# The opening of the FFN: where GpSimd forms the third pair's modulation product, and the order of the four gated tiles

## The reference

```
h = rms_norm(x) * (1 + scale) + shift          # scale, shift from ada_w, six vectors a layer
z = h @ w_up                                    # 1024 -> 2 * 3072
u, v = z[..., :3072], z[..., 3072:]
u = depthwise_conv3(u)
f = (gelu(u) * v) @ w_down                      # 3072 -> 1024
x = x + gate * rms_norm(f)
```

## Time and profile before

| | us |
|---|---|
| median of 3 runs | 2104.82 (2103.49 to 2105.01) |
| the profiled execution's own time | 2108.7 |
| its span, first to last instruction | 2106.9 |
| PE busy | 2025.1 (96%) |
| DVE busy | 1517.2 (72%) |
| POOL busy | 1295.8 (62%) |
| ACT busy | 843.0 (40%) |
| mean granted TensorE clock | 0.976 of full speed |

### The profile page before, as it was taken

The page is one execution under the profiler, slowest core; times in us unless marked ns, Lnnn a source line. Parts: engine busy times, 40 slices in busy tenths (PEclk is TensorE's granted clock), DMA queues, the critical chain, the costliest instruction groups (busy, mean ns, idle before and its releaser), DMA issues.

```text
span 2106.9 us, 26627 instructions
## 1 busy us (share of the span) xinstructions
PE 2025.1 (96%) x9048; PEld 1662.4 (79%) x9048; DVE 1517.2 (72%) x1510; ACT 843.0 (40%) x1119; POOL 1295.8 (62%) x836
## 2 busy tenths in 40 slices
PE   6899999999999999999999999799999999999996
PEld 6677776877778888888888768688888888888885
DVE  7588888978677777777777774697656665676557
ACT  4576768446322323232322355473332233222322
POOL 4534244655877877877787462368766676667653
PEclk9999999998999999999999988799999999999998
DMA  7132322531222222222222400211111111111114
GB/s 310 65 115 80 114 80 90 200 141 34 97 90 89 80 90 90 77 88 94 90 70 90 170 31 11 90 51 70 40 50 60 60 43 50 57 60 50 50 40 160
DMA packets 55931, 179.68 MB, mean 85 GB/s; under 512 B 5040, under 2 KB 6352, under 8 KB 55248
## 3 DMA queue, kind: packets, MB, share of 16 engines
q1 hardware_dynamic: 55888, 179.13, 23.8%
HBM read 166.52 MB, written 12.58 MB: 85 GB/s over the span
## 4 chain that ended last, share of the span: by engine, by line
PE 79%; DVE 7%; ACT 7%; issue 3%; POOL 3%; DMA 1%; ACTq 0%; POOLq 0%; SPq 0%; DVEq 0%
PE ps L908 38%; PE ps L587 32%; PE ps L755 3%; PE ps L1023 1%; PE ps L641 1%; PE ps L1060 1%; DVE ps L1979 1%; ACT TH L1237 1%; PE ps L689 1%; DVE sq L1838 1%; DVE Y L1918 1%; DMA ada_first<-ada 1%; ACT RA L1240 1%; ACT TH L1247 1%; ACT L1247 0%
## 5 line engine op out<-in xcount | busy, mean ns | idle before, releaser
L2100 DVE TENSOR_TENSOR Y<-Y,ps 128x1024 f32<-128x1024 f32 x336 | 406.0, 1219 | 35.6 <-PE ps L587 0.2
L1710 POOL TENSOR_TENSOR F_lo<-S,F_hi 128x1024 fp32r<-128x1024 f32 x44 | 107.0, 2431 | 328.4 <-ACT F_hi L1372 328.4
L587 PE MATMUL ps<-F_hi,WC_hi 128*128 128x512 f32 x736 | 231.8, 393 | 4.1 <-DVE Y L2100 1.6
L1124 ACT ACTIVATE So_hi<-So_raw 128x512 fp32r<-128x512 f32 x132 | 82.6, 627 | 374.3 <-POOL So_raw L1585 370.2
L587 PE MATMUL ps<-F_hi,WC_lo 128*128 128x512 f32 x736 | 230.0, 390 | 0.0
L1347 ACT ACTIVATE S<-S 128x1024 f32<-128x1024 f32 x48 | 51.0, 1062 | 442.1 <-DVE S L2204 442.0
L587 PE MATMUL ps<-F_lo,WC_hi 128*128 128x512 f32 x704 | 217.5, 390 | 0.0
L1688 POOL TENSOR_TENSOR So_lo<-So_raw,So_hi 128x512 fp32r<-128x512 f32 x132 | 187.5, 1447 | 6.1 <-ACT So_hi L1124 6.1
L587 PEld LDWEIGHTS ps<-F_hi,WC_hi 128*128 128x128 f32 x736 | 138.4, 189 | 34.8 <-DVE Y L2100 2.4
L587 PEld LDWEIGHTS ps<-F_hi,WC_lo 128*128 128x128 f32 x736 | 138.7, 188 | 29.1
L587 PEld LDWEIGHTS ps<-F_lo,WC_hi 128*128 128x128 f32 x704 | 132.7, 189 | 27.8
(11 more groups left out here) (302 smaller groups left out, 5379.8 us busy)
## 6 DMA issues: line engine op xcount, KB each, us to landing
rawA<-wA SPq DMA_DIRECT2D x62, 512.0 KB, 3.2
rawB<-wB SPq DMA_DIRECT2D x62, 512.0 KB, 3.2
E<-ada SPq DMA_DIRECT2D x46, 512.0 KB, 3.2
rawC<-wC SPq DMA_DIRECT2D x46, 512.0 KB, 3.6
quad<-ada SPq DMA_DIRECT2D x8, 2048.0 KB, 9.1
ada_first<-ada SPq DMA_DIRECT2D x4, 2048.0 KB, 15.6
outT<-X SPq DMA_DIRECT2D x16, 512.0 KB, 3.6
X<-outT SPq DMA_DIRECT2D x16, 512.0 KB, 7.1
```

The costliest lines, as they stand in the source:

```text
L587: mm = pe.matmul(out, w[:, w_cols:w_cols + P], (hi, lo)[part], start=first and w is W_hi[s] and part == 0, stop=last and w is W_lo[s])
L1124: A(dst[:, at:at + HF], src[:, src_at:src_at + HF], ACT.Copy).then_inc(op_hi, 1)
L1710: TT(dst[:], S[1][:], F_hi[:].bitcast(F32), ALU.subtract).then_inc(f_ready, 1)
L2100: TT(Y[:, m], Y[:, m], flat(ps[:, b:b + 2, :]), ALU.add).then_inc(d_added, 1)
```

## The change

On POOL, in layer 0 only, the product of unit 4 moves from behind the remainder of F in step 2 to a place between the remainders of 12 and of S2. In both layers the fourth tile set is rounded by ACT, and its remainders are formed by POOL, in the order 2, 3, 0, 1. `copy_p1` of step 2 waits for the first two of these remainders (the tiles in `acc1`) and no longer for four. Product 22 of step 2 waits for all four remainders ahead of its first matmul, where it waited for one at a time.

```diff
+        T4_ORDER = (2, 3, 0, 1)
...
                     if first and name == "22":
-                        pe.wait_ge(t4_lo, 4 * (t // UP) + k + 1)
+                        pe.wait_ge(t4_lo, 4 * (t // UP) + 4)
...
             def round_t(L, n):
 
-                for k in range(KT // 2):
+                for k in range(KT // 2) if n < 3 else T4_ORDER:
...
                 if isinstance(t, int) and t % UP == 1:
-                    act.wait_ge(t4_lo, 4 * (t // UP) + 4)
+                    act.wait_ge(t4_lo, 4 * (t // UP) + 2)
...
-                for name in READY_FIRST[:5]:
+                for name in READY_FIRST[:4]:
                     lo_of_op(name, L, 2)
-                for k in range(KT // 2):
-                    pool.wait_ge(t_hi, 16 * L + 12 + k + 1)
+                if L == 0:
+                    ada_product(4)
+                lo_of_op(READY_FIRST[4], L, 2)
+                for n, k in enumerate(T4_ORDER):
+                    pool.wait_ge(t_hi, 16 * L + 12 + n + 1)
                     TT(T_lo[3][:, k], T_raw[3][k], T_hi[3][:, k].bitcast(F32), ALU.subtract)\
                         .then_inc(t4_lo, 1)
...
-                if L == 0:
+                if L == 0 and not (static and j == 2):
                     ada_product(2 * j)
```

## The result

The changed kernel took 2109.72 us (median of 10 runs, 2104.51 to 2113.86), the kernel before 2103.88 (10 runs, 2100.46 to 2108.26): ratio 1.0031, 95% interval 1.0022 to 1.0040. Built again and timed on its own (first experiment) it gave 1.0027, interval 1.0016 to 1.0038. The forecast was 1.0016, +3.4 us. The measured time lies in its range, but the whole interval lies above the 0.2% at which I set the border of slower, to which I gave 0.26. The mechanism was right, but the sum is little more than half of the loss.

The account below looks back on a forecast made before the run. PE, busy 96% of the span, bounds the kernel; the openings' waits total 3.36 us. POOL's lateness of 2.4 plus meetings of 1.0 gave +3.4, from 2104.8 to 2108.2 us, range 2103.6 to 2111.2.

Parts of the forecast that it names:

- the sum: Whole kernel: 2.4 us of POOL lateness plus 1.0 for VectorE and POOL meeting, +3.4 us, to 2108.2.
- The load of unit 4 lands: Layer 0's opening: load lands at 529.7, 4.3 us after issue, leaving POOL idle 7.5 us ahead of the product.
- Four tiles at 5.1: POOL, step 2 of layer 0: the four tile remainders take 5.1 us, where they took 6.57 before.
- S3 0.9 late: PE, step 2 of layer 0: could start S3 at 538.42, gets it from POOL at 539.3, 0.9 us late.
- wC's remainder 2.4 late: POOL, end of layer 0's opening: wC's remainder ends at 545.3 instead of 542.9, 2.4 us later.
- VectorE's wait of 5.34 us gone: Layer 0's opening: VectorE's 5.34 us wait for unit 4's product disappears.
- No slack between 560.47 and PE's second wait: Step 3, layer 0: each microsecond POOL is late at 560.47 comes out at PE's matmul of 582.04, +2.4 there.
- The rival of the loads: Step 3, layer 0: unit 6 lands in 4.3 us, not 6.6, returning 2.3; +1.1, 2105.9 us; chance 0.17.
- A new wait ahead of product 22 of step 3: PE, step 3 of layer 0: a sign of being right, a new wait ahead of product 22; no size given.
- Layer 1 at 0: Layer 1's opening: no product moves there, so taken as 0, with bounds of -0.3 and +0.3 us.
- The meetings of VectorE and POOL: Layer 0's opening: shared SBUF ports cost POOL about 1.0 us per meeting; 0 to 2 more, taken as 1.0.
- The clock falls: Step 3: rival on the slow side, PE at half speed after longer waits; +5.9 us, 2110.7; chance 0.15.

Follow-up runs that it names:

- the control: The changed kernel with PE's step 3 of layer 0 written out ahead of its loop, same instructions; ratio 1.0014 to the kernel before, mean 2107.3 us.
- the filled one: The control plus 18 matmuls of 128x512, results unused, put where PE waits; ratio 1.0019 to the kernel before, mean 2107.7 us.
- product later still: The changed kernel with unit 4's product held until rawA for j = 3 has landed too; ratio 1.0038 to the kernel before, mean 2111.5 us.

## Why the prediction was right in kind and short in size

The steps of the sum, one by one. The load of unit 4 lands 4.7 us behind the mark: POOL started at 5.1. Four tiles at 5.1: 5.08. S3 0.9 late: 1.20, 0.98, 1.20 and 1.18 in the four profiles. wC's remainder 2.4 late: 2.8 in the changed kernel's first profile. VectorE's wait of 5.34 us gone: yes.

No slack between 560.47 and PE's second wait: not held. The remainder of 22 came 2.8, 3.7, 3.9 and 3.9 us later than in the first profile of before, but unit 6's load landed in 5.9, 5.0, 5.3 and 5.0 us instead of 6.6, so its product came only 2.1, 2.1, 2.7 and 2.4 later, and PE's matmul of 582.04 came 2.1, 2.1, 2.6 and 2.3 later (59.1, 59.2, 59.6 and 59.4 us behind the mark against 57.0). The forecast was 3.4 there. The rival of the loads, which I gave 0.17, was in part at work: 0.7 to 1.6 us came back, not the 2.3 it priced. In the second profile of before, unit 6 was issued at 38.7 behind the mark, once VectorE had summed unit 5, and not with POOL's remainder at 35.4: there the chain had slack.

A new wait ahead of product 22 of step 3: 1.60, 1.90 and 1.63 us in three of four profiles. In the first it came earlier, as the 2.38 us on v0. Layer 1 at 0: held.

The meetings of VectorE and POOL, 0 to 2 us, taken as 1.0: the first two profiles of the changed kernel show both ends. In the first, the left tap yielded (6.31 us) and POOL was held no more than before the change, 2.8 late at 22's remainder; in the second the tap took 2.58 us, POOL was held three times, and was 3.75 late. At POOL the term was thus 0 to 1.1; at PE it is hardly to be seen, because the load took it up. The rule of the Trainium skill ("SBUF — State Buffer", section "Who interferes with whom"), that one of the two holds the shared ports for a whole instruction, agrees with these rows. What they add is that the tap can stand behind four of POOL's instructions in a row (6.31 us), or get in after one (2.58 us), in executions of the same kernel; why it went one way or the other is not shown.

Altogether the five steps lost 2.8 us (159.1 in the mean of four profiles, 156.3 in the mean of two). That mean holds falls of the clock: the only two of these profiles without one, the first of each kernel, differ by 2.1 (158.2 and 156.1). At equal clock the timed runs lost 3.3 (2107.3 against 2104.0). The sum said 3.4. That this is so near the 3.3 is partly luck: the profiles show 2.1 to 2.6 us at PE's second wait, with the meetings' 1.0 taken up by the load, and no profile shows where the rest of the 3.3 lies.

So the term of the meetings was sized too large, and a larger one was missing. The step that failed is "The clock falls", which I priced as a rival at 0.15 and left out of the sum as zero. The mean granted clock went from 0.9782 (77 runs) to 0.9763 (22 runs), which at 1.42 us per 0.001 is 2.8 us: the other half of the measured 6.0. Nor was it only where I put it. I had it decided by the length of a wait in the opening, between 1.53 and 2.54 us, and only in the changed kernel; it fell there in three of four changed profiles and in one of two of before.

In the fourteen profiles the low clock varies in three stretches above all: ahead of the mark (25.4, 27.0 or 28.6 us from the first wC issue; it fell there in five profiles, of both kernels, with no wait of PE, during or right behind 32 matmuls of 128x1), in the opening, and, with the largest part, between the two FFNs, in the norms and the pooling mixer, whose code the change does not touch. From the fifth wC issue behind the mark to the last of layer 0 all fourteen took 486.3 us at clock 1.00. Between the FFNs, from the last wC issue of layer 0 to the first of layer 1 the kernel before took 220.2 and 215.7 us, the changed one 217.4, 220.6, 220.6 and 220.4; with the experiments, the three profiles without the moved product have a mean of 217.2, the eleven with it 219.7 (217.3 to 222.7). The first profiles of both kernels, from 1300 to 1345 us (granted clock third from the right, 0.72 before and 0.80 after):

```profile
1300.00:1345.00 45.00, 39.53 (x195) 35.56 (x195) 27.73 (x41) 22.34 (x37) 15.16 (x12) 0.72 0.17 59
```

```profile
1300.00:1345.00 45.00, 37.98 (x198) 33.53 (x198) 28.68 (x42) 22.67 (x35) 17.25 (x13) 0.80 0.17 59
```

The shorter mixer (217.4 us, in the changed kernel's first profile) is the one with the higher clock, as it is the fastest of its ten executions.

What stays open is why. Every kernel with the product moved has a lower mean clock than the kernel before (0.9760 to 0.9778 against 0.9782; for the control and the filled one the difference is within the noise), the one without it does not (0.9787). But profiles with nearly the same last wC issue of layer 0 (1165.9 us in two of the changed kernel) had 217.4 and 220.6 us for the mixer, and a control with the same work had 0.9778. Fourteen profiles, one to four of a kernel, are too few to tell a cause from chance here, and the clock of the timed runs is known only as a mean.

## What to carry to other kernels

Before an instruction is moved forward in an engine's queue, date its operand's arrival: here POOL stood idle for 8.7 us at the new place, and PE came 2.1 to 2.6 us later to its second wait, because in-order work stood behind it. Removing a wait is not free either where two engines share ports: an earlier PE brought VectorE's left tap into POOL's work and cost POOL 2.0 us, of which 0.9 reached the path. And where one execution differs from the next by 9 us, compare stages from a common mark, and times at equal mean clock.

## What the runs showed of the hardware

A VectorE instruction of 1.3 us that reads two SBUF tensors was held for 6.31 us by GpSimd instructions that followed each other without a pause, and got in at GpSimd's next pause (0.08 us); "product later still" shows the same with 6.35 us. The third of three 512 KB loads issued 0.6 to 0.7 us apart landed in 5.0 to 6.6 us in the kernel before and in the changed one. In the opening PE's granted clock fell to 0.50 behind waits of 1.90 to 2.43 us in eight cases and stayed at 1.00 behind five others of 1.91 to 2.38 us. Executions of one program differed in mean granted clock from 0.974 to 0.980, and in time by 1.4 us for each 0.001, so that of the kernel before, 77 runs spread over 10.8 us.
